# Moving operands of four matmul stages shifted by 8 or 16 bytes in SBUF

## What is computed

```python
for l in range(DEPTH):                                  # DEPTH = 2
    mod_p, mod_s = _adaln(cond_ctx, w_mod[l], b_mod[l]), _adaln(c, w_mod[l], b_mod[l])
    hp = _modulate(xp, norm1_g[l], ...)                 # context; the same for the latents
    if l % 2 == 0:
        qa, ka, va, qb, kb, vb = _even_heads(hp, even_w_in[j], ...)      # h @ w_in, 2048 x 4608
        ... attention ...; _even_merge(oa, ob, even_w_out[j])            # 2048 x 2048
    else:
        ... = _odd_heads(hp, odd_w_in[j], ...)                           # 2048 x 4960
        ... mLSTM, latent attention ...; _odd_merge(h, o, odd_w_out[j])  # 2048 x 2048
    x = x + gate * _conv_ffn(h, ffn_w_up[l], ..., ffn_w_down[l])         # 2048 x 11264, 5632 x 2048
```

## Time and profile before

| | before |
|---|---|
| median of three runs | 2678.48 us |
| profiled execution, its own time | 2675.88 us |
| its span from first to last instruction | 2674.1 us |
| mean granted TensorE clock | 0.976 of 2.4 GHz |
| TensorE matmul queue busy | 2550.9 us (95%) |
| TensorE weight loads busy | 2328.3 us (87%) |
| VectorE, ScalarE busy | 1485.3 us, 1295.8 us |
| DMA, mean over the span | 227 GB/s |

### The profile page before, as it was taken

How to read it: one execution, slowest core, us unless ns; L and a number is a source line. 1 busy time by engine, 2 the same in 40 slices (tenths; PEclk the granted TensorE clock), 3 DMA queues, 4 the chain that set the end, 5 groups by cost and what they waited for, 6 DMA issues and landing times. The chain is left out here.

```text
span 2674.1 us, 52531 instructions
## 1 busy us (share of the span) xinstructions
PE 2550.9 (95%) x20826; PEld 2328.3 (87%) x20826; DVE 1485.3 (56%) x1970; ACT 1295.8 (48%) x1795; POOL 11.7 (0%) x20
## 2 busy tenths in 40 slices
PE   6799999989999999999989999789899999999997
PEld 1487988878888888899989889778899999999997
DVE  1334455655454545577765445645655565567676
ACT  1443444364444444466565444334655555556553
POOL 0000000000000000000000000000000000000000
PEclk9999999989999999999989998889899999999999
DMA  9886665768888888865646884123455555555553
GB/s 388 330 317 233 231 228 184 289 256 309 318 316 319 314 318 313 321 212 192 203 128 234 321 299 142 62 93 114 156 189 186 184 187 185 185 188 187 176 186 107
DMA packets 170060, 608.28 MB, mean 227 GB/s; under 512 B 18688, under 2 KB 25152, under 8 KB 169648
## 3 DMA queue, kind: packets, MB, share of 16 engines
q1 hardware_dynamic: 168624, 600.33, 64.0%
q10 hardware_dynamic: 512, 2.97, 0.3%
q0 software_dynamic: 768, 2.79, 0.3%
HBM read 601.38 MB, written 4.63 MB: 227 GB/s over the span
## 5 line engine op out<-in xcount | busy, mean ns | idle before, releaser
L498 DVE TENSOR_TENSOR w_lo<-raw,w_hi 128x1024 fp32r<-128x1024 f32 x756 | 925.5, 1225 | 966.3 <-ACT w_hi L491 964.6
L491 ACT ACTIVATE w_hi<-raw 128x1024 fp32r<-128x1024 f32 x756 | 798.7, 1057 | 1018.2 <-PE banks L638 994.2
L636 PE MATMUL banks<-xs_ffn,w_hi 128*128 128x256 f32 x4224 | 1188.3, 281 | 5.2 <-DVE xs_ffn L792 5.0
L637 PE MATMUL banks<-xs_ffn,w_hi 128*128 128x256 f32 x4224 | 1181.9, 280 | 0.0
L638 PE MATMUL banks<-xs_ffn,w_lo 128*128 128x256 f32 x4224 | 1181.7, 280 | 0.0
L636 PEld LDWEIGHTS banks<-xs_ffn,w_hi 128*128 128x128 f32 x4224 | 797.8, 189 | 43.5 <-issue 42.6
L638 PEld LDWEIGHTS banks<-xs_ffn,w_lo 128*128 128x128 f32 x4224 | 803.8, 190 | 0.0
L637 PEld LDWEIGHTS banks<-xs_ffn,w_hi 128*128 128x128 f32 x4224 | 795.3, 188 | 0.0
L592 PE MATMUL banks<-raw,cond 128*32 128x512 f32 x1536 | 227.2, 609 | 29.2 <-DMA raw<-in_w_mod 18.0
L636 PE MATMUL banks<-xs_even,w_hi 128*128 128x256 f32 x832 | 241.8, 291 | 10.0 <-DVE w_lo L498 5.9
L637 PE MATMUL banks<-xs_even,w_hi 128*128 128x256 f32 x832 | 233.3, 280 | 0.0
(11 more groups left out here) (305 smaller groups left out, 2054.2 us busy)
## 6 DMA issues: line engine op xcount, KB each, us to landing
raw<-in_w_mod SPq DMA_DIRECT2D x384, 512.0 KB, 6.7
raw<-in_ffn_w_up SPq DMA_DIRECT2D x352, 512.0 KB, 3.5
raw<-in_ffn_w_down SPq DMA_DIRECT2D x176, 512.0 KB, 4.1
raw<-in_even_w_in SPq DMA_DIRECT2D x72, 512.0 KB, 4.0
raw<-in_odd_w_in SPq DMA_DIRECT2D x64, 512.0 KB, 4.5
raw<-in_even_w_out SPq DMA_DIRECT2D x32, 512.0 KB, 3.7
raw<-in_odd_w_out SPq DMA_DIRECT2D x32, 512.0 KB, 3.2
raw<-in_odd_w_tail SPq DMA_DIRECT2D x8, 448.0 KB, 3.7
```

The lines of the kernel that those rows point to most:

```text
L491: act.activation(w_hi[:, o % SPLIT], raw[:, s % RAW], ACT.Copy).then_inc(hi_done.sem, 1)
L498: dve.tensor_tensor(w_lo[:, o % SPLIT], raw[:, s % RAW], w_hi[:, o % SPLIT].bitcast(F32), ALU.subtract).then_inc(lo_done.sem, 1)
L636: pe.matmul(made, hi, x_hi, start=start and not second, stop=False, skip_group_check=second)
L637: pe.matmul(made, hi, x_lo, start=False, stop=False, skip_group_check=second)
```

## The change

A helper allocates the moving operand's tile with 8 more float32r columns (32 bytes) and takes its view from column `first` on. In FFN 1 and in the odd layer's stage an otherwise unused tile of 56 columns (224 bytes) is laid before it.

```diff
+        def moving_tiles(name, scope, first):
+            wide = sb(name, [P, KD * 2 * NT + 8], F32R, scope)
+            return wide[:, first:first + KD * 2 * NT].rearrange("p (k n) -> p k n", k=KD)
...
                 acts = sb(f"acts{l}", [P, KF, NT], scope=scope)
-                xs = sb(f"xs_ffn{l}", [P, KD, 2 * NT], F32R, scope)
+                if l:
+                    pad = sb("pad_ffn", [P, 56], scope=scope)
+                xs = moving_tiles(f"xs_ffn{l}", scope, (2, 6)[l])
...
-                xs = sb("xs_even", [P, KD, 2 * NT], F32R, scope)
+                xs = moving_tiles("xs_even", scope, 4)
...
-                            xs = sb("xs_odd", [P, KD, 2 * NT], F32R, inner)
+                            pad = sb("pad_odd", [P, 56], scope=inner)
+                            xs = moving_tiles("xs_odd", inner, 4)
```

## The result

The changed kernel is slower: a median of 2737.2 us (2733.5 to 2738.5, four runs) against 2676.9 us (2651.6 to 2679.6, four runs), a ratio of 1.026 with a 95% interval of 1.020 to 1.032. The profiled execution of after spans 2735.7 us, 61.6 us more than the 2674.1 of before, at the same mean granted clock (0.977 against 0.976).

A forecast was written before the change was run, and what follows sets the result against it. TensorE was taken as the bound: in four stages, 17,088 matmuls times their start-to-start spacing. Shifted distances were valued at 0, so the forecast was 2676 us, the profiled execution's own time, range 2629 to 2712.

The forecast's parts named there:

- one price: Four stages: the only cost counted is what 17,088 matmuls do at the new distance of moving operand from weights.
- neither end: Four stages: neither the 45.9 us gain nor the 29.9 us loss was taken; the effect was put at 0.
- either rhythm: Matmul start-to-start spacings read from the kernel before: quick, 113.3 ns, and slow, 117.8 ns, a difference of 4.44 ns.
- All slow: Four stages: every matmul at 117.8 ns because 113.3 needs the present distance; loss 29.9 us, 2706 us; chance 0.15.
- The floor: Four stages: no spacing below 113.3 ns, as no row of 256 fp32r columns was below 113.
- A third rhythm: Both FFN stages at 122 ns per matmul, 13.3 ns more per three products; 75.6 us, 2751 us; chance 0.10.
- One side quick: Four stages: distances above or below -64 give 113.3 ns, the other side 117.8; 2666 or 2669 us; chance 0.12.
- All quick: Four stages: all at 113.3 ns since 117.8 needs a distance of just -64; gain 45.9 us, 2630; chance 0.15.
- Line crossings: FFN stages (+8, -8): 65 lines of 16 bytes read, not 64; 1.67 ns per matmul, 21 us, 2697; chance 0.07.
- What would show it: The prediction's list of signs, read per stage from the count of matmuls in windows at full clock.
- The caution on FFN 1: FFN 1: its spacing by itself tells nothing, since one interruption sets whether it runs at 113.3 or 117.8 ns.
- the quick form: FFN 1: the forecast's second form, distance does not choose and FFN 1 falls into 113.3 ns; 2648.3 us; chance 0.10.

The follow-up runs named there:

- the control: Kernel before with the change's helper but no operand shifted, only the tiles behind the operands moved by 256 bytes: 2650.0 us, before on the same chip 2650.9.

## Why the prediction was wrong

**The frame held.** The prediction put the time of the four stages as matmuls times spacing and said that there is one price. The count is unchanged, the waits are unchanged to within a few us, the four stages hold the 61.6 us, and the control shows that the moved tiles on VectorE and ScalarE are worth nothing, as costed.

**The step that failed** is the sentence "I take neither end: a shift of 8 or 16 bytes leaves both rhythms possible, and interruptions choose, as before. Value: 0." It measured 61.6 us: no stage with a shifted operand has either rhythm. With 8 bytes there is one, 120.0 ns; with +16 interruptions still choose, but between 116.7 and some 119 ns; with -16 it is 119.2. So the term that was put at 0 had no row behind it: the addresses decide which rhythms there are, and the interruptions only choose among those. What stood behind it was the reading of the nearest rows, "So both rhythms turn up on either side, never a third one with 256 columns, and -64 alone has both." The rows that I took for other distances are, modulo 256, only two: -192 is +64, and the rest are -64 and +64. Modulo 512, the step of the operands, they looked like three. And +64 has both rhythms as well: the key-value projection and 69 stretches of even are slow, the odd tail's first group, with its narrow loads, and five stretches of even quick. The starts in these rows are multiples of 64 bytes on both operands, so none of them bore on 8 or 16 bytes. The row that did move in steps of 4, va in the earlier trace rows, is plain fp32, whose columns go at half the rate, as the prediction noted itself; a stream at half the rate told nothing of this one.

**The ceiling was no ceiling.** "All slow" gave 29.9 us and set the top of the range, and the result lies 25 us above it. The floor held: no kernel has a mean spacing below 113.3 in these stages.

**The rivals.** *A third rhythm*, at 0.10, was right in kind: a spacing above both. Its size was off, since I copied the step of 13.3 ns; it measures 360.0 - 353.3 = 6.7 ns, that is 120.0 for a matmul and not 122, but it also took in even and odd, which the rival had left alone: 61.6 us and not 75.6. *One side quick* fell: +8 and -8 both give 120.0, and neither +16 nor -16 has the quick rhythm. *All quick* fell for this change; that the slow rhythm can be got rid of is true, but by moving both operands. *All slow* fell, since the rhythms of before aren't the ones that remain.

*Line crossings* is half right. The place was: a moving operand that starts off a multiple of 16 bytes costs. The Trainium skill, "SBUF — State Buffer", section "SBUF: two separate sides", lets one expect a price there, with its 16-byte lines and a penalty for each access that crosses to a new one. For the weights alone no such price is shown. The size was not right: 1.67 ns for each matmul on top of either rhythm was the estimate, 115 ns in the quick one; measured are 120.0, which is 6.7 above the quick rhythm and 2.2 above the slow one, and 121.7 for 4 bytes. A fixed price for one more line would be the same for 4 and for 8. And the 16-byte shifts, which cross no further line, cost 3.2 ns in even and 4.2 in odd.

**What would show it** worked as written: "A spacing off both values refutes the forecast at once", and 120.0 in the first window of FFN 0 did. The sign "A stage with a single rhythm through all its interruptions means that it does" held for FFN 0, but even, at +16, kept alternating, although the distance had changed both of its values. The caution on FFN 1 was in place: of 16 runs of before on one chip 14 took 2647 to 2655 us and two 2673 to 2674, about the 27 us of one rhythm of FFN 1, though no trace of those runs shows it. Counted from the quick form, the control's span of 2648.2 us, the change costs 2735.7 - 2648.2 = 87.5 us and not 61.6; the 26 us between the two counts are the luck of which rhythm FFN 1 of the profiled execution of before fell into.

**What stays open.** What inside the chip makes the spacing is not shown. That a matmul's reads of the moving operand and the next weight load's reads get in each other's way would suit a rule in two addresses, and the weights' address alone moved the query projection's spacing; but no record shows a read. The Trainium skill, "SBUF — State Buffer", section "Who interferes with whom", has TensorE read the two operands through independent ports and wait for nobody; whatever the reason, these runs have 113.3 to 120.0 ns with nothing but the addresses changed. Why a slow start falls back to the quick rhythm on odd multiples of 16 bytes is open too, and so are the distances between those of the table, which weren't tried.

## What to carry to other kernels

Where matmuls of few columns stream against a fresh weight load each, take the byte address of the moving operand relative to the weights as a tuning parameter: keep both starts on multiples of 16 bytes, try the distance in steps of 16 or 32 modulo 256, and try moving both together, which gave this tuned kernel 0.7% (16 bytes, distance -64). Read the spacing from the count in a window at the full clock; the duration of a matmul hid a 3% change (116.3 to 120.1 ns over both FFN stages) behind 1%. And before rows are taken as neighbours of an untried address, reduce them by every period that they could have: rows that differ by a whole period are one.

## What the hardware showed that I had not expected

- Spacing between matmuls of 256 fp32r columns depends on both start addresses; the distance counts modulo 256 bytes wherever that was tried (-80, -72, -64, 0, +64, 128): 113.3 ns at best, 120.0 at equal places, 121.7 with the moving operand 4 bytes off a multiple of 16.
- At one and the same pair of addresses on multiples of 32 two rhythms hold for long stretches (113.3 and 117.8 ns, FFN 1 for 700 us); at +16 bytes there are two others (116.7 and some 119 ns). With both on odd multiples of 16, at -64, a slow start fell back to the quick rhythm after at most 13 matmuls, in three kernels.
- Moving the weights by 8 or 16 bytes slowed the query projection, whose own operand had not moved, from 113.3 to 117.5 and 118.2 ns.
